# Fourier mixing folded by symmetry in tokens and frequencies, and another order of TensorE fills and modulation blocks inside the attention loop

## The chip, the cores and the metric

The kernel runs on one core of one Trainium2 chip. The metric is the device time of one execution in microseconds (us). Engine names are those of the profile: PE is TensorE (PEld its weight loads), DVE is VectorE, ACT is ScalarE, POOL is GpSimd, SP the engine that issues most transfers. L957 is line 957 of the kernel before.

## What is computed

A transformer block with mixture-of-experts, followed by two state-space layers, all in float32. Only one piece of the first block matters here:

```
hl = modulate(rms_norm(x, g), shift, scale)        # 512 tokens x 1024
pl = hl @ w_in                                     # q, k, v (512 wide each) and f (512 wide)
attention: 4 heads, each q block of 128 tokens against 768 keys, difference of two softmaxes
fourier_mix(f):
    fg = f.reshape(b, n, 4, 128)                   # 4 groups of 128 channels
    fr = fft2(fg, axes=(tokens, channels), norm='ortho').real
    return einsum('bngc,gcd->bngd', fr, w_fourier)
x = x + gate * (concat([attention, fourier]) @ w_out)
```

For real input, the real part of the two-dimensional transform is the sum of cosine times cosine and minus sine times sine. A cosine over the 512 tokens is even about token 256, a sine odd; the same holds of the result's frequencies.

## The kernel before

Activations lie features-major: 128 partitions of features by 512 tokens. The kernel is one block of hand-ordered instruction streams, one for each engine, joined by semaphores; each engine runs its stream in order, so a wait holds everything behind it.

**The attention loop** has 16 iterations n = 0 to 15 (head n // 4, query block n % 4). In each one:

- PE runs `scores(n)` (L931, 4 matmuls into banks 2 to 5), which waits until ACT has taken the exponentials of n - 1. Then come the two halves of `turn_weights(n - 1)` (L943, three 128x128 transposes each), and between and behind them **fills**: projections of the values and of the Fourier features (`values`, `to_mix`, both L840, 8 matmuls of 512 columns), the Fourier work, a head's `head_values` (L957, 3 matmuls in each of two iterations), its `head_norm_sum` (L964), and the start of the output projection (`out_part`, L969).
- DVE runs `maxima(n)` (L2234 and L2237), which waits for the scores; two **modulation blocks** (`mod_block`, L2230); `attention_weights(n)` (L2242, L2244, L2248), which waits for ACT's exponentials; and a third block. In some iterations there is also a head's evacuation (`head_out`, L2252), its variance (`head_var`, L2256) or its scaling (`head_scale`, L2260 and L2263, a reciprocal over 512 columns).
- ACT takes the exponentials (L1664) and copies PE's results out of PSUM (`copy`, L1553), in a fixed order, with a square root (L1682) for a head's norm where n = 8, 12 and after the loop.

**Modulation blocks** compute the conditioning vector of the second block: 48 blocks of 128 rows by 1024, each one a multiply with accumulation on DVE over 512 KB of weights. Two buffers hold them. POOL issues a block's load (L613) as soon as DVE has used the block two before it. The rule is three blocks in each iteration.

**The ring** holds projection weights in two slots of 2 MB. SP refills a slot (L427) as soon as PE is done with it; in the loop these are the two slots of the output projection's weights, the first one free after `values(5)` (n = 3), the second after `to_mix(3)` (n = 7).

**Fourier work of a group g**: `mix_channels` (L900) multiplies 4 token tiles by a 128x256 table of cosines and sines; ACT copies the two banks; `mix_tokens` (L908 and L909) sums over the 4 token tiles, 8 matmuls of 512 columns; ACT copies; `mix_out` (L916) applies the group's weights. It stands in n = 8 to 14.

After the loop come the last head, the output projection, the router and the experts. The loads of the expert weights start when the last head's values are done (`pv_mm`) and all 48 blocks are used (`ada_used`).

Of the kernel before, what the change touches and what calls it, by code (L numbers as in the profile page):

```python
# [19 lines left out]
ALU = mybir.AluOpType  # L20
# [3 lines left out]
P = 128  # L24
D = 1024
KC = D // P
T = 512
TC = T // P
# [57 lines left out]
def build(nc, A, out):  # L86

    with ExitStack() as ctx:
# [53 lines left out]
        dft_c, dft_s, dft_ch = wk(13312, TC, T), wk(15360, TC, T), wk(17408, 256)  # L142
        fab, fre = wk(17664, 2, 4, 256), wk(19712, T)
# [114 lines left out]
        B_BANKS = (0, 2, 0, 2, 5, 2, 5, 5)  # L258
        SCATTER_BANKS = (7, 4)
# [43 lines left out]

        def f32r(v):

            return bass.AP(twins[v.tensor.name][v.offset // TWIN], v.offset % TWIN, [(TWIN, P), *v.ap[1:]])
# [24 lines left out]
        fourier_mm, fourier_evac = sem("fourier_mm"), sem("fourier_evac")  # L331
        AB, FR, FO = 2, 3, 4
# [5 lines left out]
        zero_row_stored, route_mm = sem("zero_row_stored"), sem("route_mm")  # L338
# [75 lines left out]
        def _(sp):  # L414
# [34 lines left out]
            for name, tile in (("rope_c", rope_c), ("rope_s", rope_s), ("dft_c", dft_c), ("dft_s", dft_s),  # L449
# [8 lines left out]
                         zeros[0:1, :].unsqueeze(1).broadcast_to([1, 4, 256])).then_inc(zero_row_stored, 16)  # L458
# [9 lines left out]
            for n in range(TILES_E):  # L468
# [9 lines left out]
                elif n == 8:  # L478
                    sp.wait_ge(routing_evac, 5)
                    sp.dma_start(h_rows[0:T, :].rearrange("(t p) d -> p t d", p=P), tok_rows).then_inc(rows_stored, 16)  # L480
                    sp.wait_ge(rows_stored, 16)
# [118 lines left out]
        def _(pool):  # L600
# [15 lines left out]
            pool.wait_ge(zero_row_stored, 16)  # L616
            pool.wait_ge(rows_stored, 16)
# [98 lines left out]
        def _(pe):  # L716
# [174 lines left out]
            def mix_channels(g):  # L891
                if g:
                    pe.wait_ge(fourier_evac, 4 * (g - 1) + FR)
                else:
                    pe.wait_ge(in_mix, 16 * 6)
                    pe.wait_ge(qkv_evac, 22)
                for t in range(TC):
                    if g and t == 2:
                        pe.wait_ge(fourier_evac, 4 * (g - 1) + FO)
                    mm = nc.tensor.matmul(PS[:, t // 2, (t % 2) * 256:(t % 2 + 1) * 256], fT[:, g, t * P:(t + 1) * P],  # L900
                                          dft_ch, start=True, stop=True)
                    if t % 2:
                        mm.then_inc(fourier_mm, 1)

            def mix_tokens(g, tiles):
                pe.wait_ge(fourier_evac, 4 * g + AB)
                for t in tiles:
                    nc.tensor.matmul(PS[:, 0, :], fab[:, g % 2, t, 0:P], dft_c[:, t, :], start=(t == 0), stop=False)  # L908
                    mm = nc.tensor.matmul(PS[:, 0, :], fab[:, g % 2, t, P:2 * P], dft_s[:, t, :], start=False,  # L909
                                          stop=(t == TC - 1))  # L910
                if t == TC - 1:
                    mm.then_inc(fourier_mm, 1)

            def mix_out(g):
                pe.wait_ge(fourier_evac, 4 * g + FR)
                nc.tensor.matmul(PS[:, 1, :], wfour[:, g, :], fre, start=True, stop=True).then_inc(fourier_mm, 1)  # L916
# [58 lines left out]
            for n in range(HEADS * TC):  # L975
                hd, qc = n // TC, n % TC
                scores(n)
                if n in (9, 11, 12, 14):
                    mix_out({9: 0, 11: 1, 12: 2, 14: 3}[n])
# [7 lines left out]
                elif n == 1:  # L987
                    values(2)
                    values(3)
                elif n == 2:  # L990
                    values(4)
                elif n == 3:
                    values(5)
                    tile_done()
                    tile_wait("in", 1, 1)
                elif n < 8:
                    to_mix(n - 4)
                    if n == 7:
                        tile_done()
                elif n in (8, 9, 11, 12):  # L1000
                    mix_channels({8: 0, 9: 1, 11: 2, 12: 3}[n])
                elif n in (10, 13):
# [2045 lines left out]
```

## Time and profile before

| | |
|---|---|
| median of 3 runs | 2228.44 us (2226.58 to 2231.45) |
| the profiled execution | 2228.12 us |
| its span, first to last instruction | 2226.4 us |
| granted TensorE clock, mean | 0.991 |
| PE busy / DVE busy / ACT busy | 96% / 54% / 32% |
| attention loop, first scores to the last turn of weights | 117.7 to 294.8 us |

The profile is of one execution. Its span is 1.7 us shorter than that execution's device time; what lies around the span is taken as unchanged. Matmuls overlap in the list of instructions, so the time of one in a stream is read from the start of the next one, or from the chain of waits, whose pieces do not overlap.

### The profile page before, as it was taken

The page shows a single profiled execution, that of the slowest core. Times are in us where ns is not written, and L with a number is a line of the kernel's source. Part 1 is how long each engine was busy: PE and PEld are TensorE (multiplying, and loading weights), DVE is VectorE, ACT ScalarE, POOL GpSimd, SP SyncE. Part 2 cuts the span into 40 slices and gives each one's busy share as a digit, 9 for nine tenths or more (in the row PEclk, how much of TensorE's full clock was granted, in tenths as well). Part 3 has the DMA queues.
Part 4 walks back from the last instruction along what each step waited for, and adds up shares of the span by engine and source line. Part 5 has one row for each costly group of instructions (what it writes and reads, how often), then busy time and mean ns, then how long its engine had stood idle before and what let it go on. Part 6 is the DMA issues. An engine that isn't in the chain of part 4 may idle for free.

```text
span 2226.4 us, 24806 instructions
## 1 busy us (share of the span) xinstructions
PE 2136.7 (96%) x9914; PEld 1429.5 (64%) x9914; DVE 1211.9 (54%) x1726; ACT 702.7 (32%) x1059; POOL 154.2 (7%) x157
## 2 busy tenths in 40 slices
PE   7999998997999989999999999999999999999998
PEld 3444444333333336678888888877777788888886
DVE  1876853344443336894465555576876545343434
ACT  4123422110000006223332232256785424231321
POOL 0011100003210014000000000000110000000000
PEclk9999999999999999999999999999999999999999
DMA  9756464999999992212354545314342222222221
GB/s 389 288 188 214 144 253 188 414 427 427 420 427 426 426 422 93 77 67 76 132 180 151 184 162 182 125 57 129 113 148 86 95 78 93 95 94 94 94 95 57
DMA packets 112808, 434.71 MB, mean 195 GB/s; under 512 B 7982, under 2 KB 13106, under 8 KB 98760
## 3 DMA queue, kind: packets, MB, share of 16 engines
q1 hardware_dynamic: 92872, 361.46, 42.4%
q0 software_dynamic: 19840, 71.93, 9.0%
q8 instruction: 66, 1.08, 0.2%
q14 instruction: 30, 0.25, 0.0%
HBM read 430.57 MB, written 6.36 MB: 196 GB/s over the span
## 4 chain that ended last, share of the span: by engine, by line
PE 58%; PEld 14%; DVE 8%; issue 7%; DMA 6%; ACT 3%; DVEq 2%; POOL 1%; POOLq 0%; SPq 0%; PEldq 0%; ACTq 0%
PE PS L1132 8%; PE PS L740 6%; PE PS L743 6%; PE PS L744 6%; PE PS L840 6%; PEld PS L740 4%; PEld PS L744 4%; PEld PS L743 4%; PE PS L1155 4%; DMA work<-in_w_dn 3%; PE PS L1399 2%; PE PS L1403 2%; PE PS L1402 2%; PE PS L1169 2%; PE PS L969 2%
## 5 line engine op out<-in xcount | busy, mean ns | idle before, releaser
L744 PE MATMUL PS<-work_f32r,work_f32r 128*128 128x512 f32 x1168 | 454.4, 389 | 0.0
L2155 DVE TENSOR_TENSOR ring_f32r<-ring,work_f32r 128x2048 fp32r<-128x2048 f32 x100 | 227.8, 2287 | 140.5 <-ACT work_f32r L1553 140.1
L740 PE MATMUL PS<-work_f32r,work_f32r 128*128 128x512 f32 x768 | 299.5, 390 | 2.0 <-DVE work_f32r L2900 1.0
L743 PE MATMUL PS<-work_f32r,ring_f32r 128*128 128x512 f32 x768 | 298.8, 389 | 0.0
L1553 ACT ACTIVATE work_f32r<-ring 128x2048 fp32r<-128x2048 f32 x100 | 190.3, 1910 | 303.1 <-DMA ring<-in_mlp_w 246.6
L744 PEld LDWEIGHTS PS<-work_f32r,work_f32r 128*128 128x128 f32 x1168 | 219.2, 188 | 45.7
L1132 PE MATMUL PS<-work 128*64 128x512 f32 x752 | 171.2, 598 | 1.7 <-ACT work L1761 1.7
L740 PEld LDWEIGHTS PS<-work_f32r,work_f32r 128*128 128x128 f32 x768 | 144.2, 188 | 33.1 <-DVE work_f32r L2900 1.5
L743 PEld LDWEIGHTS PS<-work_f32r,ring_f32r 128*128 128x128 f32 x768 | 144.2, 188 | 30.0 <-issue 0.2
L740 PE MATMUL PS<-h_f32r,work_f32r 128*128 128x512 f32 x400 | 155.9, 390 | 1.5 <-DVE work_f32r L2175 1.5
L743 PE MATMUL PS<-h_f32r,ring_f32r 128*128 128x512 f32 x400 | 155.6, 389 | 0.0
L2472 DVE SCALAR_TENSOR_TENSOR x<-PS,mod,x 128x512 f32<-128x512 f32 x128 | 90.2, 746 | 68.7 <-PE PS L1169 68.3
L1771 ACT ACTIVATE work<-PS 128x256 f32<-128x256 f32 x32 | 12.3, 383 | 357.7 <-PE PS L1132 357.7
L2717 DVE SCALAR_TENSOR_TENSOR x<-PS,mod,x 128x512 f32<-128x512 f32 x64 | 48.1, 751 | 137.0 <-PE PS L744 136.9
L1399 PE MATMUL PS<-h_f32r,work_f32r 128*128 128x512 f32 x288 | 122.4, 425 | 0.0
L1132 PEld LDWEIGHTS PS<-work 128*64 128x64 f32 x752 | 51.6, 137 | 101.6 <-issue 101.6
L1553 ACT ACTIVATE work<-PS 128x512 f32<-128x512 f32 (+2 forms) x94 | 50.8, 550 | 198.5 <-PE PS L840 85.8
L1402 PE MATMUL PS<-h_f32r,ring_f32r 128*128 128x512 f32 x288 | 113.3, 393 | 0.0
L1403 PE MATMUL PS<-work_f32r,work_f32r 128*128 128x512 f32 x288 | 113.3, 393 | 0.0
L2708 DVE TENSOR_SCALAR work<-PS 128x512 f32<-128x512 f32 x64 | 43.9, 691 | 116.3 <-PE PS L744 116.2
L1155 PE MATMUL PS<-work 128*64 128x512 f32 x384 | 94.9, 611 | 9.1 <-DMA work<-in_w_dn 8.4
L1925 ACT ACTIVATE work_f32r<-work 128x512 fp32r<-128x512 f32 x64 | 40.4, 631 | 171.8 <-DVE work L2708 171.8
(423 smaller groups left out, 3358.7 us busy)
## 6 DMA issues: line engine op xcount, KB each, us to landing
work<-in_w_gu SPq DMA_DIRECT2D x47, 2048.0 KB, 20.4
ring<-in_mlp_w SPq DMA_DIRECT2D x64, 1024.0 KB, 5.1
work<-in_w_dn SPq DMA_DIRECT2D x24, 2048.0 KB, 23.7
ring<-in_w_gu SPq DMA_DIRECT2D x16, 2048.0 KB, 24.8
work<-in_ada_w_2T POOLq DMA_DIRECT2D x48, 512.0 KB, 3.6
work<-in_ada_w_2T POOLq DMA_DIRECT2D x16, 1536.0 KB, 6.8
ring<-in_m_w_in SPq DMA_DIRECT2D x20, 1024.0 KB, 5.1
work<-in_w_adaT POOLq DMA_DIRECT2D x8, 2048.0 KB, 10.3
```

The costliest lines, as they stand in the source:

```text
L740: mm = nc.tensor.matmul(PS[:, bank + k, :], f32r(w_of), f32r(hi(c)), start=first and c == 0, stop=False)
L743: nc.tensor.matmul(PS[:, bank + k, :], f32r(wlo), f32r(hi(c)), start=False, stop=False)
L744: mm = nc.tensor.matmul(PS[:, bank + k, :], f32r(w_of), f32r(lo(c)), start=False, stop=last and c == 3)
L840: mm = nc.tensor.matmul(PS[:, bank, 0:n], cols_of(c), rhs_of(c), start=(c == 0), stop=(c == KC - 1))
L1132: mm = nc.tensor.matmul(PS[CAP * half:CAP * (half + 1), 2 + s, :], xbT[:, 4 * part + c, CAP * s:CAP * (s + 1)], w[:, c, half * 512:(half + ...
L1155: mm = nc.tensor.matmul(PS[CAP * s:CAP * (s + 1), 5 + n, :], hidT[:, s, k % 2, CAP * (k // 2):CAP * (k // 2 + 1)], tiles[s][0][:, k, n * 5 ...
L1399: mm = nc.tensor.matmul(PS[:, k, :], f32r(w_of), f32r(h[:, c, :]), start=(c == 0), stop=False)
L1402: nc.tensor.matmul(PS[:, k, :], f32r(wlo), f32r(h[:, c, :]), start=False, stop=False)
L1403: mm = nc.tensor.matmul(PS[:, k, :], f32r(w_of), f32r(xbc_h_lo[:, c, :]), start=False, stop=(c == KC - 1))
L1553: return nc.scalar.activation(out, in_, ACT.Copy)
L2155: tt(f32r(ring[:, s, at, :]), ring[:, s, at, :], f32r(tiles[s][:, at, :]), ALU.subtract).then_inc(w_split, 1)
L2472: stt(x[:, c, :], PS[:, SCATTER_BANKS[c % 2], :], mod1[:, 5 * KC + c:5 * KC + c + 1], x[:, c, :], ALU.mult, ALU.add).then_inc(x2_added, 1)
```

## The change

- **Tokens folded.** After a group's features are projected, DVE forms for the token pairs (t, 512 - t) the difference into `f_odd` and the sum in place (`fold_tokens`, two operations of 255 columns, one operand read backwards, and a copy of token 256). PE then transforms only 2 tiles of sums by cosines and 2 tiles of differences by sines, with token 256 added by one more matmul: 5 matmuls of 128 columns.
- **Frequencies folded.** `mix_tokens` computes only the cosine sum at 257 frequencies and the sine sum at 255: 3 matmuls of 257 columns and 2 of 255. ACT copies the first, and DVE makes frequencies 1 to 255 as their sum and 257 to 511 as their difference (`unfold_frequencies`, two operations of 255 columns, one written backwards). `mix_out` waits for this instead of for ACT's copy.
- **Fills in another order.** n = 1 held two value projections, now one; n = 1 to 4 hold values 2 to 5, n = 5 to 8 the four Fourier projections, and n = 9 to 12 one Fourier group each, with `mix_out` of a group in the next iteration. Three matmuls of the output projection move from n = 15 to n = 13.
- **Modulation blocks in another order**: 2, 3, 3, 3, 4, 5, 5, 4, 1, 3, 3, 2, 0, 3, 4, 3 for n = 0 to 15 (before, 3 each), at most two of them ahead of `attention_weights`. `fold_tokens` stands behind `maxima` in n = 6 to 9, `unfold_frequencies` at the end of n = 9 to 12.
- The tables of the token transform are smaller (386 KB and 255 KB instead of 1024 KB each). A store of a zero row signals on another semaphore.

The diff, cut to its core:

```diff
@@ TensorE
             def mix_channels(g):
+                pe.wait_ge(folded, g + 1)
                 if g:
-                    pe.wait_ge(fourier_evac, 4 * (g - 1) + FR)
+                    pe.wait_ge(fourier_evac, 3 * (g - 1) + FO)
...
-                for t in range(TC):
-                    mm = nc.tensor.matmul(PS[:, t // 2, (t % 2) * 256:(t % 2 + 1) * 256], fT[:, g, t * P:(t + 1) * P],
-                                          dft_ch, start=True, stop=True)
+                even, odd, cosines, sines = fT[:, g, :], f_odd[:, g, :], dft_ch[:, 0:P], dft_ch[:, P:2 * P]
+                for t in range(2):
+                    nc.tensor.matmul(PS[:, 0, t * P:(t + 1) * P], even[:, t * P:(t + 1) * P], cosines, start=True, stop=True)
+                nc.tensor.matmul(PS[:, 0, 3 * P:4 * P], odd[:, P:2 * P], sines, start=True, stop=True)
+                nc.tensor.matmul(PS[:, 0, 2 * P:3 * P], odd[:, 0:P], sines, start=True, stop=False)
+                nc.tensor.matmul(PS[:, 0, 2 * P:3 * P], f_half[:, g, :], cosines, start=False, stop=True).then_inc(fourier_mm, 1)
+            def mix_tokens(g):
+                pe.wait_ge(fourier_evac, 3 * g + AB)
+                if g:
+                    pe.wait_ge(folded, GROUPS + g)
+                for t in range(3):
+                    nc.tensor.matmul(PS[:, 1, 0:257], fab[:, g % 2, t, :], dft_c[:, t, :], start=(t == 0), stop=(t == 2))
+                for t in range(2):
+                    mm = nc.tensor.matmul(PS[:, 1, 257:512], fab[:, g % 2, 2 + t, :], dft_s[:, t, :], start=(t == 0), stop=(t == 1))
             def mix_out(g):
-                pe.wait_ge(fourier_evac, 4 * g + FR)
+                pe.wait_ge(folded, GROUPS + g + 1)
@@ ScalarE
-                if n in (8, 9, 11, 12):
-                    mixed_channels({8: 0, 9: 1, 11: 2, 12: 3}[n])
+                if FIRST_MIX <= n < FIRST_MIX + GROUPS:
+                    mixed_channels(n - FIRST_MIX)
                 exps(n)
@@ VectorE
+            def fold_tokens(g):
+                dve.wait_ge(qkv_evac, 18 + g + 1)
+                early, late = fT[:, g, 1:T // 2], mirrored(fT[:, g, T // 2 + 1:T])
+                tt(f_odd[:, g, 1:T // 2], early, late, ALU.subtract)
+                nc.vector.tensor_copy(f_half[:, g, 0:1], fT[:, g, T // 2:T // 2 + 1])
+                tt(early, early, late, ALU.add).then_inc(folded, 1)
+            def unfold_frequencies(g):
+                dve.wait_ge(fourier_evac, 3 * g + UV)
+                early, late, odd = fre[:, 1:T // 2], mirrored(fre[:, T // 2 + 1:T]), PS[:, 1, 257:512]
+                tt(late, early, odd, ALU.subtract)
+                tt(early, early, odd, ALU.add).then_inc(folded, 1)
+            BLOCKS_AT = (2, 3, 3, 3, 4, 5, 5, 4, 1, 3, 3, 2, 0, 3, 4, 3)
...
-                mod_block(3 * n)
-                mod_block(3 * n + 1)
+                first, count = sum(BLOCKS_AT[:n]), BLOCKS_AT[n]
+                ahead = min(2, count) if n else 0
+                for q in range(first, first + ahead):
+                    mod_block(q)
                 attention_weights(n)
-                mod_block(3 * n + 2)
+                for q in range(first + ahead, first + count):
+                    mod_block(q)
                 if hd >= 2 and qc == 0:
                     head_scale(hd - 2)
+                if FIRST_MIX <= n < FIRST_MIX + GROUPS:
+                    unfold_frequencies(n - FIRST_MIX)
```

Two places show what moves. The first is DVE in iteration n = 12, from its maxima to the next iteration's. Before (the rows with `mod` are modulation blocks, `norm_buf` is the head's variance and reciprocal):

```order
L2234 TENSOR_REDUCE sm<-PS 128x2
L2237 TENSOR_SCALAR sm<-sm 128x2
L2256 TENSOR_SCALAR norm_buf<-PS 128x512
L2230 SCALAR_TENSOR_TENSOR work,mod<-work,cond 128x1024 x2
L2242 RECIPROCAL sm<-sm 128x2
L2244 TENSOR_SCALAR work<-work,sm 128x768
L2248 SCALAR_TENSOR_TENSOR work<-work,sm 128x768
L2230 SCALAR_TENSOR_TENSOR work,mod<-work,cond 128x1024
L2260 RECIPROCAL norm_buf<-norm_buf 128x512
L2263 SCALAR_TENSOR_TENSOR h<-work,sm,norm_buf 128x512
```

and of the change:

```order
L2222 TENSOR_REDUCE sm<-PS 128x2
L2225 TENSOR_SCALAR sm<-sm 128x2
L2244 TENSOR_SCALAR norm_buf<-PS 128x512
L2230 RECIPROCAL sm<-sm 128x2
L2232 TENSOR_SCALAR work<-work,sm 128x768
L2236 SCALAR_TENSOR_TENSOR work<-work,sm 128x768
L2248 RECIPROCAL norm_buf<-norm_buf 128x512
L2251 SCALAR_TENSOR_TENSOR h<-work,sm,norm_buf 128x512
L2263 TENSOR_TENSOR work<-work,PS 128x255
L2264 TENSOR_TENSOR work<-work,PS 128x255
```

The three blocks have left this iteration, and group 3's unfold stands behind the head's scaling.

The second is PE from `scores(12)` to `scores(13)`. Before (L931 scores, L916 mix out, L943 transposes, L900 channels, L908 and L909 tokens):

```order
L931 MATMUL PS<-work 128x512 x2
L931 MATMUL PS<-work 128x256 x2
L916 MATMUL PS<-work 128x512
L943 MATMUL PS<-mats_sb,work 128x128 x3
L900 MATMUL PS<-work 128x256 x4
L943 MATMUL PS<-mats_sb,work 128x128 x3
L908 MATMUL PS<-work 128x512
L909 MATMUL PS<-work 128x512
L908 MATMUL PS<-work 128x512
L909 MATMUL PS<-work 128x512
L931 MATMUL PS<-work 128x512 x2
```

and of the change, up to the next iteration's mix out (L922), which waits for the unfold above:

```order
L937 MATMUL PS<-work 128x512 x2
L937 MATMUL PS<-work 128x256 x2
L922 MATMUL PS<-work 128x512
L949 MATMUL PS<-mats_sb,work 128x128 x3
L905 MATMUL PS<-work 128x128 x2
L906 MATMUL PS<-work 128x128
L907 MATMUL PS<-work 128x128
L908 MATMUL PS<-work 128x128
L949 MATMUL PS<-mats_sb,work 128x128 x3
L915 MATMUL PS<-work 128x257 x3
L917 MATMUL PS<-work 128x255 x2
L937 MATMUL PS<-work 128x512 x2
L937 MATMUL PS<-work 128x256 x2
L922 MATMUL PS<-work 128x512
```

All of a group's token sums now stand in its own iteration, and between them and the next `mix_out` there is only one `scores`.

## Rows read from the trace of the kernel before

**Rows 1.** By stretch: length, busy of PE, PEld, DVE, ACT, POOL, clock, DMA, GB/s.

```profile
212.90:275.20 62.30, 60.35 (x207) 30.28 (x206) 49.91 (x67) 30.73 (x57) 9.14 (x17) 1.00 0.48 167
275.20:294.80 19.60, 19.31 (x62) 8.74 (x62) 17.05 (x28) 7.43 (x16) 3.44 (x7) 1.00 0.56 189
400.00:600.00 200.00, 188.00 (x854) 73.33 (x853) 84.53 (x180) 26.14 (x57) 34.46 (x24) 0.98 1.01 425
```

**Rows 2.** Chain of waits, PE pieces: start, us, what (two records a matmul).

```profile
187.48 2.58 PE PS L957 x6
203.77 6.88 PE PS L840 x16
212.97 1.49 PE PS L931 x8
214.94 1.74 PE PS L900 x8
216.71 0.61 ACT work L1553
225.98 1.05 PE PS L916 x2
```

**Rows 3.** Chain of waits, pieces on DVE, the transfers and ACT.

```profile
163.38 3.51 DMA work<-in_ada_w_2T
168.44 7.98 DMA work<-in_ada_w_2T
...
262.16 1.88 ACT work L1664 x4
...
267.23 3.26 DVE norm_buf L2260
...
294.83 0.52 PE PS L943 x3
```

**Rows 4.** PE groups by shape, first 350 us: xcount | busy us, mean ns.

```profile
L840 PE MATMUL PS<-work,ring 128*128 128x256 f32 x64 | 14.1, 379 | 0.0
L729 PE MATMUL PS<-ones 128*128 128x128 f32 x32 | 4.7, 289 | 0.1
```

**Rows 5.** DVE in order of time: start, us, engine, line, what [idle before].

```profile
57.72 2.77 DVE L2132 TENSOR_TENSOR work<-work,norm_buf 128x256 f32<-128x256 f32 x8
141.13 1.75 DVE L2234 TENSOR_REDUCE sm<-PS 128x2 f32<-128x1536 f32 x1
143.04 1.22 DVE L2230 SCALAR_TENSOR_TENSOR work<-work,cond 128x1024 f32<-128x1024 f32 x1
146.15 0.16 DVE L2242 RECIPROCAL sm<-sm 128x2 f32<-128x2 f32 x1
148.09 1.22 DVE L2230 SCALAR_TENSOR_TENSOR work<-work,cond 128x1024 f32<-128x1024 f32 x1
224.50 3.35 DVE L2260 RECIPROCAL norm_buf<-norm_buf 128x512 f32<-128x512 f32 x1
228.60 1.75 DVE L2234 TENSOR_REDUCE sm<-PS 128x2 f32<-128x1536 f32 x1
```

**Rows 6.** The block loads: issue to landing, all 48; and DVE's first block.

```profile
DMA to landing us min/median/max: 3.4/3.6/8.0
134.99 1.22 DVE L2230 SCALAR_TENSOR_TENSOR work<-work,cond 128x1024 f32<-128x1024 f32 x1 [2.06 <-DMA work<-in_ada_w_2T]
```

**Rows 7.** PE in order of time: `scores` of iteration 5.

```profile
177.12 1.56 PE L931 MATMUL PS<-work 64*128 64x512 f32 x8
```

**Rows 8.** Issues in order of time: SP's ring load, POOL's first blocks, ACT's table load.

```profile
167.33 44.52 SPq L427 DMA_DIRECT2D ring<-in_w_out  x4
131.02 1.45 POOL L613 DMA_DIRECT2D work<-in_ada_w_2T  x2 [23.35 <-DVE work L2141]
219.46 1.28 ACT L1682 ACT_TABLE_LOAD   x1
```

**Rows 9.** Waits, first 350 us: us in total, times, longest.

```profile
DVE work L2230 <- DMA work<-in_ada_w_2T: 18.0, 15, 3.7
```

More of the change, by code:

```diff
@@ L914, in mix_out @@
             def mix_out(g):
-                pe.wait_ge(fourier_evac, 4 * g + FR)
-                nc.tensor.matmul(PS[:, 1, :], wfour[:, g, :], fre, start=True, stop=True).then_inc(fourier_mm, 1)
+                pe.wait_ge(folded, GROUPS + g + 1)
+                nc.tensor.matmul(PS[:, 0, :], wfour[:, g, :], fre, start=True, stop=True).then_inc(fourier_mm, 1)
             def scores(n):
@@ L977, in _ @@
                 scores(n)
-                if n in (9, 11, 12, 14):
-                    mix_out({9: 0, 11: 1, 12: 2, 14: 3}[n])
+                if FIRST_MIX < n <= FIRST_MIX + GROUPS:
+                    mix_out(n - FIRST_MIX - 1)
                 if n:
@@ L986, in _ @@
                     values(1)
[L987 to L998, printed above, removed]
-                        tile_done()
-                elif n in (8, 9, 11, 12):
-                    mix_channels({8: 0, 9: 1, 11: 2, 12: 3}[n])
-                elif n in (10, 13):
-                    mix_tokens({10: 1, 13: 3}[n], range(2, 4))
+                elif n < 5:
+                    values(n + 1)
+                    if n == 4:
+                        tile_done()
+                        tile_wait("in", 1, 1)
+                elif n < FIRST_MIX:
+                    to_mix(n - 5)
+                    if n == 8:
+                        tile_done()
+                elif n < FIRST_MIX + GROUPS:
+                    mix_channels(n - FIRST_MIX)
+                elif n == 13:
+                    tile_wait("out", 0, 0)
+                    pe.wait_ge(fourier_evac, 3 * 2 + FO)
+                    out_part(0, 1, OUT_ORDER[0:3])
                 elif n == 14:
-                    tile_wait("out", 0, 0)
                     pe.wait_ge(head_done, 2)
+                    pe.wait_ge(fourier_evac, 3 * 3 + FO)
                     out_part(0, 0, OUT_ORDER[0:5])
                 elif n == 15:
-                    pe.wait_ge(fourier_evac, 4 * GROUPS)
-                    out_part(0, 1, OUT_ORDER[0:6])
+                    out_part(0, 1, OUT_ORDER[3:6])
                 if n:
@@ L1017, in _ @@
                     head_values(hd - 1, 3, KCH)
-                if n in (8, 11):
-                    mix_tokens({8: 0, 11: 2}[n], range(4))
-                elif n in (9, 12):
-                    mix_tokens({9: 1, 12: 3}[n], range(2))
+                if FIRST_MIX <= n < FIRST_MIX + GROUPS:
+                    mix_tokens(n - FIRST_MIX)
                 elif n == 15:
@@ L2269, in _ @@
                     modulation((5, ADA_TILES // 2), -MOD_EARLY // 4, cond1, col("b_ada", 0, 48), mod1)
-                    attention_weights(0)
-                    for q in range(3):
-                        mod_block(q)
-                    continue
+                    nc.vector.memset(f_odd[:, :, 0:1], 0.0)
+                    nc.vector.memset(f_half, 0.0)
+                if FIRST_MIX - 3 <= n < FIRST_MIX + 1:
+                    fold_tokens(n - FIRST_MIX + 3)
                 if hd >= 2 and qc == 0:
```

81 lines of the change are left out of this document (32 added, 49 removed).

## The prediction

> **What bounds the kernel now.** I read the busy time by stretch first. In the Fourier part of the loop (212.9 to 275.2 us) PE is busy 60.4 of 62.3 us, and DVE already 49.9; in the stretch behind it 19.3 and 17.1 of 19.6 [rows 1]. So PE is full, but DVE has a fifth of its time free at most. The chain of waits says the same more sharply: up to 261 us it runs almost only over PE pieces [rows 2], then over DVE, ACT's exponentials and block loads until the last turn of weights at 294.83 [rows 3]. The last three iterations are thus bound by DVE and its loads, with PE just kept fed. Further on, the experts stream their weights at 425 GB/s with the transfer engines at 1.01 [rows 1]; these loads begin when the loop's last values and blocks are done. No part of the rest depends on absolute time, so what the loop gains or loses is what the kernel gains or loses. Everything comes down to one number: when the last turn of weights (now 294.83) starts.
>
> **What PE saves.** A full matmul of 512 columns costs 0.86 us (8 in 6.88, 3 in 2.58), one of 256 columns 0.43 (4 in 1.74) [rows 2]. Before, a group takes 4 x 0.43 + 8 x 0.86 = 8.6 us before its `mix_out`. After, it takes 2.2 us for the tokens (3 of 257 and 2 of 255 columns; 256 columns in a long row cost 14.1 / 32 = 0.44) and 5 of 128 columns, 4.7 / 16 = 0.29 each, 1.5 us [rows 2, 4]. That is 4.9 us less per group, 19.8 us for four. For the small ones the price is bounded by 0.29 (same weights again) and the 0.43 of twice the columns, so 1.5 to 2.2 us; I take 1.5.
>
> **What DVE gets.** In start-to-start times DVE's pieces are: `maxima` 1.9, a block 1.15, `attention_weights` 1.94 (146.15 to 148.09), `head_scale` 4.1 (224.50 to 228.60) [rows 5]. A two-operand operation over 256 columns costs 2.77 / 8 = 0.35 [rows 5]. A fold is two of these and a tiny copy, 0.8 us; an unfold 0.7; together 6 us in the loop. No row shows an operand read or written backwards: below, a forward one at 0.35 is the floor; above, I take 1.0 us, one third of the 3.26 of the slowest pass over 512 columns, the reciprocal [rows 3], scaled to 255 with a margin down since it is no division. I take 0.35, the row of the same operation.
>
> **What the blocks can do.** There are two buffers. From the end of a block to the start of the one two later it takes 0.3 us to POOL's issue and 3.4 to 3.6 to the landing, a **trip** of 3.8 us [rows 3, 6]. Two blocks per iteration are always there; more than two wait for trips. So five blocks cost two trips: an iteration with five takes at least 1.9 + 0.8 + 3 x 1.15 + 2 x 3.8 = 13.8 us on DVE, while PE needs 1.49 (scores) + 0.7 (turns) + 6.88 (projection) + 2.58 (values) = 11.7 [rows 2]. DVE falls behind just where the change puts the most blocks.
>
> **The walk.** M(n) is when DVE starts `maxima(n)`.
> - `scores(5)` started at 177.12 [rows 7]. It comes one projection of 6.9 us earlier, less about 0.5 of waiting for `attention_weights(1)`, and ends near 172.4: M(5) = 172.4.
> - n = 5: the ring slot frees when `values(5)` ends, and SP's load starts with it, as at 167.33 before [rows 8]. Then a block load issued just behind took 8.0 us instead of 3.5 [rows 3]. Now this lands in an iteration with five blocks: the first starts at 179.2; with three blocks and two trips M(6) = 190.2.
> - n = 6: as above, 13.8. M(7) = 204.0.
> - n = 7: 1.9, fold 0.8, `head_out` 0.6, a block, a trip, two blocks: 10.6. M(8) = 214.6. PE also idles some 4 us here, as `head_norm_sum` needs this late `head_out`.
> - n = 8: ACT's square root stands behind the copies of the last projection, which is late too: `head_scale` begins at 222.3. M(9) = 226.4, 5 us behind its scores.
> - n = 9: 1.9, fold, two blocks, a trip, a block, unfold: M(10) = 235.9. PE has reached `mix_out(0)` at 231.6 and waits 4 us.
> - n = 10: PE-bound: `mix_out` 1.0, a wait for its copy 0.4, channels 1.5, turns 0.7, values 2.58, tokens 2.2, scores 1.49 [rows 2]: 10.0. M(11) = 245.9.
> - n = 11: a loop without slack: `mix_out` 1.0, copy 0.6, channels 1.5, copy 0.6 (216.71), exponentials 1.88, weights 1.94, unfold 0.7, handoffs 0.5: 8.8 [rows 2, 3]. M(12) = 254.7. (ACT takes group channels before the exponentials.)
> - n = 12: the same up to the exponentials, then square root with table load 1.9 (1.28 of it the load [rows 8]), `head_scale` 4.1, unfold: 13.1. M(13) = 267.8; PE idles 5 us before `mix_out(3)`.
> - n = 13: `mix_out`, two copies, table load, exponentials, weights, a block: 8.5. M(14) = 276.3. n = 14: four blocks, 9.9. M(15) = 286.2. n = 15: maxima, `head_out`, two blocks (one on a trip), weights: done at 293.1.
>
> The same walk over the order of before ends 1.1 us too early against the trace, mostly in n = 13 to 15; I have already put that in by rounding each step up. So 294.83 becomes 293.1: a gain of 1.7 us. Of the 19.8 us that PE saves, some 18 turn into waits for DVE. Other edits cost nothing: the smaller tables land before 60 us, where PE waits for none of them; the row store's semaphore is passed long before it is used. The sum is 2228.12 - 1.7 = **2226.4 us**, against the profiled execution, which lies 0.3 under the median. A measurement of this kernel can tell about 0.2% (4.5 us) from no change, so this is no change.
>
> On the trip, the Trainium skill ("DMA: Bandwidth & Descriptors", Anatomy of one DMA) gives 2.0 us plus the bytes at 436 GB/s. For 512 KB that is an estimate of 3.2 us where the rows show 3.4 to 3.6 [rows 6]; by it the trip would be 3.5 and the walk end 3 us earlier, at 2223.6.
>
> **The rivals.**
> - *The ring load doesn't collide.* The first of the five blocks' loads is issued about a microsecond from the ring load's start; a little earlier and it lands before. Then n = 5 costs 4.4 us less, all of it on the walk: 2222.0. Against it: the same engine order gave 8.0 us before. For it: the margin is under 1 us, and the walk has other steps that I rounded up.
> - *PE is the bound.* DVE is busy 54% of the span and PE 96%; if DVE's lateness is absorbed, all 19.8 us come through: 2208.3. For it: the PE row of the stretch, and that PE hardly waited before. Against it: the last iterations already hang on DVE [rows 3], and the DVE work of n = 5 to 15 (97 us by the pieces above, without trips) is as long as PE's (99). The Trainium skill says to improve the most-contended engine ("Perfetto Trace Analysis", Identifying the Most-Contended Engine); by occupancy that is PE here, and by that rule this rival is the forecast.
> - *Slower: the trip gets longer.* Where blocks are taken back to back, two loads are always in flight. At the loop's start POOL issued two at 131.02, and the first was used at 134.99, 3.97 later, not 3.5 [rows 6, 8]. About twelve trips lie one behind another on the walk, so each 0.1 us costs 1.2 us. From a trip of 4.3 us on the kernel is measurably slower; at 4.4 it is 2233.6. Against it: before, pairs issued 1.15 apart landed in 3.5.
> - *Slower: backwards operands.* At 1.0 us instead of 0.35 for each of the 16 operations the walk grows by 8.9 us: 2235.3. It decides from about 0.8 us each.
>
> **How the numbers follow.** The walk's result 0.50 (its own range 2223.7 to 2231.5, from the small matmuls' upper price of +2.8 and a trip 0.1 to 0.2 us off); no collision or a part of the lateness absorbed 0.23; PE the bound 0.10; longer trips 0.13; slow backwards operands 0.04. Faster by over 0.2%: 0.33, within 0.50, slower 0.17. The range leaves out the PE-bound case and the far end of the slow ones: 2217 to 2233.
>
> **What would show it.** Right: PE idle of some 15 us in n = 7 to 13, with the releaser DVE, at `head_norm_sum(0)`, `mix_out(0)` and `mix_out(3)`; DVE waits for block loads well over the 18.0 us of before [rows 9], one of some 5 us near 174 to 179; iterations n = 5 and 6 17 to 18 and 14 us long on DVE. Wrong: PE over 97% busy from 212 on; scores of n = 6 to 9 followed at once by their maxima; folds or unfolds over 0.5 us an operation; trips of other than 3.8 us; or a last turn of weights before 289 or after 298.

## The result, and the profile after

| | before | after |
|---|---|---|
| median, 20 runs each | 2228.57 us (2226.55 to 2232.54) | 2233.8 us (2229.82 to 2237.77) |
| the profiled execution / its span | 2228.12 / 2226.4 | 2237.49 / 2235.5 |
| mean granted clock | 0.991 | 0.983 |
| last turn of weights | 294.83 | 302.32 |

The ratio is 1.0021 (95% interval 1.0014 to 1.0027): slower by 0.2%. The forecast was 2226.4 in a range of 2217 to 2233, so the time lies just outside it, 7.4 us above the forecast. The profiled execution of after is a late one of its own kernel, 3.7 us over the median, and its mean clock of 0.983 is among the lowest of the 20 (their median is 0.985); what it shows of single places is real, but its sum is larger than that of a typical run. That will matter below. Nor is the rest of the kernel quite fixed: from the last turn of weights to the end of the span it took 1931.6 us in the profile before, 1933.2 after, and 1928.6 to 1935.9 in all fourteen profiles of this study. A gain read at the last turn of one profile is therefore not yet a gain of the kernel; for that the medians count.

Busy time by stretch, after, the same three stretches as [rows 1] (length, busy of PE, PEld, DVE, ACT, POOL, clock, DMA share, GB/s):

```profile
212.90:275.20 62.30, 51.07 (x198) 28.50 (x197) 48.77 (x72) 24.79 (x48) 6.61 (x12) 0.88 0.43 143
275.20:294.80 19.60, 19.60 (x62) 9.27 (x61) 13.44 (x22) 8.08 (x15) 3.30 (x6) 0.91 0.43 142
400.00:600.00 200.00, 188.42 (x860) 73.18 (x858) 81.80 (x176) 26.53 (x58) 33.69 (x24) 0.98 1.00 424
```

PE had 60.4 us of work in the first stretch before and has 51.1 now, part of it at a slower clock: it idles 11 us. The experts' stretch is what it was. The kernel is no longer bound by PE in the loop.

The chain of waits of after, some pieces (start, us, what). Before, it ran mostly over PE up to 261 us [rows 2], except for DVE and two block loads from 159.95 to 179.76 [rows 3]; now block loads stand in it from the start of the loop:

```profile
130.40 5.00 DMA work<-in_ada_w_2T
...
136.96 4.36 DMA work<-in_ada_w_2T
...
169.35 4.58 DMA work<-in_ada_w_2T
...
175.49 8.16 DMA work<-in_ada_w_2T
...
197.09 3.57 DMA work<-in_ada_w_2T
...
202.22 3.49 DMA work<-in_ada_w_2T
...
211.84 2.07 PE PS L970 x2
...
227.59 3.35 DVE norm_buf L2248
231.03 0.77 DVE h L2251
231.93 5.46 PE PS L963 x6
...
244.82 4.98 DMA work<-in_ada_w_2T
...
271.99 0.75 DVE h L2251
...
273.46 2.07 PE PS L922 x2
...
289.15 4.80 DMA work<-in_ada_w_2T
```

Two things stand out. Loads of 512 KB that took 3.5 us take 4.4 to 5.0 in several places, and 8.2 once, beside the ring load. And one `head_norm_sum` (L970) and one `mix_out` (L922) take 2.07 us where 1.05 is normal [rows 2], three matmuls of `head_values` (L963) 5.46 instead of 2.58.

The waits of the loop, 117 to 300 us (us in total, times, longest), against 18.0 us for block loads before [rows 9]:

```profile
DVE work L2218 <- DMA work<-in_ada_w_2T: 23.4, 20, 4.5
PE PS L970 <- ACT work L1675: 5.8, 2, 4.1
PE PS L922 <- DVE work L2264: 5.6, 2, 5.0
PE PS L949 <- DVE work L2236: 4.1, 3, 1.9
PE PS L963 <- DVE h L2251: 3.4, 1, 3.4
```

The last four are idles of PE, and behind the longest one of each line the granted clock is low. Four windows that begin with the first matmul after the idle (the clock is the third number from the end), and the loop as a whole:

```profile
211.84:217.40 5.56, 5.56 (x14) 2.38 (x14) 3.65 (x7) 0.33 (x1) 1.51 (x3) 0.50 0.57 189
231.93:237.20 5.27, 5.27 (x7) 2.17 (x8) 5.12 (x11) 2.25 (x5) 0.73 (x2) 0.50 0.27 103
273.46:276.00 2.54, 2.54 (x6) 1.40 (x7) 2.46 (x3) 0.43 (x1) 0.00 (x0) 0.50 0.00 0
144.60:153.60 9.00, 8.94 (x20) 4.00 (x21) 8.00 (x12) 2.36 (x5) 1.71 (x3) 0.81 0.59 211
117.70:302.30 184.60, 161.68 (x529) 78.66 (x527) 141.14 (x224) 62.84 (x127) 27.02 (x48) 0.94 0.50 171
```

0.50 is the lower of PE's two levels, 1.2 GHz. Before, the clock was 1.00 in all of 117.7 to 294.8. So this kernel pays an idle of PE twice: once for the wait, and again for the 2.7 us by which norm sum, scores and a turn are longer at 211.84, or the 2.9 us of `head_values` at 231.93 (5.46 instead of 2.58). The Trainium skill ("TensorE: Matmul & The Clock Gate", A second HAM failure mode: psum-queue depth-cycling) says as much: waits between bursts throw the clock back, and the throughput suffers though each matmul at full clock is as fast as ever. It also calls the number of slow matmuls at a kernel's start variable from run to run (What's actually happening). The place of a fall varied here too, between kernels: with four buffers, below, the same idle before `head_values(1)` was followed by the full clock (three matmuls in 2.81 us), and a shorter one before `mix_out(0)` by the low one:

```profile
221.32 2.81 PE L965 MATMUL PS<-work 128*128 128x512 f32 x6 [3.39 <-DVE h L2254]
...
229.90 2.04 PE L924 MATMUL PS<-work 128*128 128x512 f32 x2 [2.10 <-DVE work L2267]
```

The length of a single idle thus does not settle by itself what the clock does behind it.

### The profile page after: what moved, and what is told of

Read it like the earlier page. It is cut to its first block, busy times and chain, and to the rows that moved or that the text cites. A ratio compares the mean times of both kernels' runs of the same rounds, so it can differ in the third digit from the quotient of the medians.

```text
span 2235.5 us, 24794 instructions
## 1 busy us (share of the span) xinstructions
PE 2131.7 (95%) x9898; PEld 1431.6 (64%) x9898; DVE 1218.0 (54%) x1748; ACT 699.5 (31%) x1055; POOL 153.8 (7%) x157
## 4 chain that ended last, share of the span: by engine, by line
PE 55%; PEld 15%; DVE 9%; issue 7%; DMA 7%; ACT 3%; DVEq 2%; POOL 1%; POOLq 0%; SPq 0%; PEldq 0%; ACTq 0%
PE PS L1133 8%; PE PS L745 6%; PE PS L748 6%; PE PS L749 6%; PEld PS L745 5%; PEld PS L749 5%; PEld PS L748 4%; PE PS L845 4%; PE PS L1156 4%; DMA work<-in_w_dn 3%; PE PS L1400 2%; PE PS L1404 2%; PE PS L1403 2%; PE PS L1170 2%; PE PS L975 2%
## 5 line engine op out<-in xcount | busy, mean ns | idle before, releaser
L1554 ACT ACTIVATE work<-PS 128x512 f32<-128x512 f32 (+3 forms) x90 | 47.5, 539 | 195.2 <-PE PS L845 75.9
## 6 DMA issues: line engine op xcount, KB each, us to landing
ring<-in_w_gu SPq DMA_DIRECT2D x16, 2048.0 KB, 23.4
```

Of the source, the lines that this page charges most:

```text
L1554: return nc.scalar.activation(out, in_, ACT.Copy)
```

## The experiments

All twelve kernels were run beside the kernel before, whose medians in them lay between 2228.2 and 2229.8 us. "Under after" compares medians of different batches of runs. Where the ratios to the kernel before give another difference it is named, and a difference of under some 2.5 us between two of these kernels is not clear of the intervals.

**Keeping the clock.** Ahead of the longest waits of PE stand small matmuls on ones, in a free bank.

```diff
+                    if n in (1, HEADS * TC - 1):
+                        keep_warm(6, 6 if n == 1 else 5)
                     pe.wait_ge(a_ready, n + 1)
...
+                if hd == 0:
+                    keep_warm(1, 12)
                 pe.wait_ge(osq_ready, hd + 1)
...
+                        if hd == 1:
+                            keep_warm(1, 11)
                         pe.wait_ge(head_done, hd)
...
+                if g == GROUPS - 1:
+                    keep_warm(0, 16)
                 pe.wait_ge(folded, GROUPS + g + 1)
```

> The changed kernel with dummy 128-column matmuls before five of PE's waits (the turn of weights 1 and 15, the norm sum of head 0, the values of head 1, the mix out of group 3), so that PE does not stand idle there. Theory: the waits themselves cost what the walk says, and the 9 us by which the loop ends later than the walk come from the granted TensorE clock of 0.5 behind each of these waits; the kernel gets 4 to 8 us faster, the clock stays at 1.0 in the loop, and the last turn of weights starts near 295. Rival: VectorE sets the pace anyway, and the slow matmuls lie beside its work; no change within 1 us. Second rival: the dummies push real work back by up to 1 us and nothing is won.

Measured: 2232.93 us (12 runs), ratio to before 1.0010 (0.9999 to 1.0021). In its profile the clock is 1.00 from 117 to 200 and 0.98 from 200 to 290 (0.98 and 0.89 in after's), and the last turn comes at 297.79, 4.5 us earlier than in after's profile. But the median is only 0.9 us better (2.5 by the ratios, and the two intervals overlap). The profile of after is of a run with more clock lost than its median run. So the clock's price is 4 to 6 us between these two profiles (4.5 at the last turn, 5.9 in the length of the loop) and an estimated 1 to 2.5 in a typical run, as long as the kernel also waits for its blocks; block waits did not fall (24.7 us).

**Four block buffers instead of two.** The kernel before has no room for them; the smaller tables of the change free it. The semaphores of the two added buffers, and the later counts on them, are left out here.

```diff
-        ..., [wk(26624, D), wk(27648, D)]
+        ..., [wk(17664, D), wk(18688, D), wk(26624, D), wk(27648, D)]
...
-                pool.wait_ge(ada_used, 2 + ADA_LATE + max(q - 1, 0))
-                pool.dma_start(ada_block[q % 2], ...).then_inc(ada_loaded[q % 2], 16)
+                pool.wait_ge(ada_used, 2 + ADA_LATE + max(q - 3, 0) if q > 1 else 2)
+                pool.dma_start(ada_block[q % 4], ...).then_inc(block_loaded[q % 4][0], 16)
```

> The changed kernel with four buffers for modulation blocks instead of two, same order. Theory: VectorE falls behind in iterations 4 to 7 because five blocks cost two round trips of 3.8 us (4.9 us for the second load of a pair); with four buffers its waits for block loads fall from 24 us to under 6, PE's idle before the norm sum of head 0 goes from 4.1 to about 1, and the kernel gets 8 to 14 us faster (the walk without clock loss gives 8, the rest is clock). Rival: VectorE's own work, not the loads, is what is late; under 3 us.

Measured: 2222.18 us (8 runs), 0.9968 (0.9957 to 0.9979): 11.6 us less than after, and faster than before. Waits, 117 to 300 us:

```profile
PE PS L924 <- DVE work L2267: 7.1, 2, 5.0
PE PS L965 <- DVE h L2254: 3.4, 1, 3.4
DVE work L2221 <- DMA work<-in_ada_w_2T: 1.7, 2, 1.4
```

Of 23.4 us of block waits 1.7 are left, and `head_norm_sum(0)` waits 0.88 us instead of 4.09. The idles before `mix_out(3)` and `head_values(1)` are as long as in after (L924 is `mix_out`, L965 `head_values`), and one of 2.1 before `mix_out(0)` is new.

**Three blocks in every iteration, in the changed kernel**, `BLOCKS_AT = (3,) * 16`.

> The changed kernel with three modulation blocks in each iteration, as before the change. Theory: the order of the blocks costs, since five in a row wait for loads; by the walk it is worth 1.5 us, and 3 to 6 with the clock. But three blocks in iterations 8 and 12, where the head's scaling stands, delay the unfold and make PE's waits there longer, so a loss of up to 3 us is the other side. Rival: the order of blocks was right and this is 3 us slower or more.

Measured: 2229.28 us (12 runs), 0.9999 (0.9990 to 1.0007). Without the new order of blocks, the sum of all that folding and new fills gain and cost is nothing. DVE waits for blocks 14.6 us.

**The new order of blocks alone, in the kernel before.**

> The kernel before with only the new order of modulation blocks (2, 3, 3, 3, 4, 5, 5, 4, 1, 3, 3, 2, 0, 3, 4, 3), no fold and the old fills. Theory: the walk gives 5 to 7 us slower than before, since with five blocks the round trips make VectorE late and PE waits. Rival: with the unfolded Fourier work PE has enough to cover it, within 1.5 us of before.

Measured: 2235.05 us (8 runs), 1.0032 (1.0018 to 1.0045). The same table of numbers costs 5 to 7 us here and 4.5 to 5 in the changed kernel, by the run above. DVE waited 27.3 us for blocks instead of the 18.0 of [rows 9].

**Short trips, before and after.** The question left was whether a trip weighs more now than it did. 46 of the 48 loads bring 8 KB instead of 512, in both kernels.

```diff
+                cols = D if q < 2 else 16
-                pool.dma_start(ada_block[q % 2], A["ada_w_2T"][0, q * P:(q + 1) * P, :]) ...
+                pool.dma_start(ada_block[q % 2][:, 0:cols], A["ada_w_2T"][0, q * P:(q + 1) * P, 0:cols]) ...
...
-                stt(w, w, 1.0, cond2[:], ...
+                stt(w, w, 0.0, cond2[:], ...
```

> The kernel before with short trips: of 48 block loads the first two are whole, the other 46 bring 16 columns of each row (8 KB instead of 512 KB), and the blocks multiply by 0, so the second block's conditioning vector is its bias alone. Same instructions, two buffers, same order; a trip gets shorter by up to the 1.5 to 2 us that the bytes take. Theory (the kernel before has PE as its bound up to 261 us and hides its trips; only the last iterations hang on them): a gain of 1 to 4 us, 2225 to 2228.5. Rival (DVE waits for loads cost before as much as after): a gain like that of the changed kernel with the same edit.

> The changed kernel with the same edit (46 of 48 block loads bring 16 columns of each row, blocks multiply by 0, so the second block's conditioning vector is its bias alone). Two buffers, the change's own order of blocks. Theory (the folded kernel hangs on trips of 3.8 to 5 us, some twelve of them on its chain in n = 1 to 11): the waits for blocks fall from 24.0 to some 10 us, and 8 to 12 us come back, 2222 to 2226, so that with short trips the change is faster than the kernel before by 2 us or more, the other way round than with the real ones. Rival (the idles and clock of PE cost the change, not the loads): under 4 us come back.

Measured: before 2227.02 (10 runs), 0.9992 (0.9982 to 1.0002); after 2222.14 (7 runs), 0.9971 (0.9960 to 0.9983). The same edit is worth 1.9 us before (its interval still includes no change) and 11.7 after (11.1 by the ratios). DVE's waits fell by about as much in both. First the kernel before, with the transfers (KB each, median us from issue to landing):

```profile
DVE work L2231 <- DMA work<-in_ada_w_2T: 3.1, 2, 2.1
...
work<-in_ada_w_2T POOLq DMA_DIRECT2D x46, 8.0 KB, 1.9
```

and the changed one:

```profile
DVE work L2219 <- DMA work<-in_ada_w_2T: 5.6, 5, 1.4
...
work<-in_ada_w_2T POOLq DMA_DIRECT2D x46, 8.0 KB, 1.9
```

15 us of DVE waits vanish in the one and 18 in the other, with gains of 1.9 and 11.7: before, PE's work covers nearly all of them, after, about a third. This is the central measurement of the study. Shorter loads also take traffic off the transfer engines (the ring load's median landing falls from 9.2 to 6.3 us), but four buffers, which leave every load whole, come to the same time (2222.18), so it is the trip that counts. On the landing of 1.9 us for 8 KB the trace agrees with the fixed part of about 2 us that the Trainium skill gives ("DMA: Bandwidth & Descriptors", Anatomy of one DMA).

**No arithmetic in folds and unfolds.** Each keeps a copy of one column and its signal.

```diff
-                tt(f_odd[:, g, 1:T // 2], early, late, ALU.subtract)
-                nc.vector.tensor_copy(f_half[:, g, 0:1], fT[:, g, T // 2:T // 2 + 1])
-                tt(early, early, late, ALU.add).then_inc(folded, 1)
+                nc.vector.tensor_copy(f_half[:, g, 0:1], fT[:, g, T // 2:T // 2 + 1]).then_inc(folded, 1)
...
-                tt(late, early, odd, ALU.subtract)
-                tt(early, early, odd, ALU.add).then_inc(folded, 1)
+                nc.vector.tensor_copy(late[:, 0:1], odd[:, 0:1]).then_inc(folded, 1)
```

> The change without the arithmetic of the folds and unfolds on DVE: the two additions of each are left out, a copy of one column stays and signals, and the two buffers are zeroed once in iteration 0, so the Fourier half of the output is not that of the reference. The small matmuls, the order of fills and blocks stay. Eight folds and unfolds of some 0.75 us each, 6 us of DVE work in the loop. If DVE is the bound throughout n = 5 to 12, 4 to 6 us of it come back: 2228 to 2230. If the block loads are the bound (a trip hides a fold behind a load), 1 to 3 us come back: 2231 to 2233.

Measured: 2232.76 us (12 runs), 1.0021 (1.0011 to 1.0031): 1.0 us under after, at the near end of the second case, and by the ratios (1.0021 for both) nothing. The folds are not what costs the change its gain.

**The norms' steps reordered.** Head 0's square root no longer stands behind a projection's copy, and group 3's unfold stands ahead of head 1's scaling.

```diff
@@ ScalarE
                 elif n < FIRST_MIX:
+                    if n == 8:
+                        head_root(0)
                     projected(13 + n)
...
-                if hd >= 2 and qc == 0:
-                    head_root(hd - 2)
                 if FIRST_MIX <= n < FIRST_MIX + GROUPS:
                     mixed_tokens(n - FIRST_MIX)
+                if n == 12:
+                    head_root(1)
@@ VectorE
-                if hd >= 2 and qc == 0:
-                    head_scale(hd - 2)
                 if FIRST_MIX <= n < FIRST_MIX + GROUPS:
                     unfold_frequencies(n - FIRST_MIX)
+                if hd >= 2 and qc == 0:
+                    head_scale(hd - 2)
```

> The change, with two steps of the heads' norms reordered, same work. On ACT the square root of head 0 stands ahead of the last projection's copy in iteration 8 (before, behind it and behind the turned weights), and the square root of head 1 behind the copy of group 3's token sums in iteration 12; on DVE the unfold of group 3 stands ahead of the scaling of head 1. Theory (PE's idles in front of head_values(1), 3.4 us, and mix_out(3), 5.0 us, and the lower clock behind them are a part of what the change lost): both idles go or fall under 1 us, the last turn of weights comes 4 to 8 us earlier than the 302.3 of the change's profile, and the time falls by 3 to 7 us, to 2227 to 2231. Rival (DVE's chain of blocks and trips sets the end whatever PE's idles do): DVE starts its next maxima at the same moments, the idles move elsewhere, and the time stays within 1.5 us of 2233.8.

Measured with two buffers: 2232.16 us (12 runs), 1.0010 (1.0001 to 1.0018), 1.6 us under after (2.5 by the ratios, the intervals overlap), less than I expected. The idle before `mix_out(3)` fell to 0.56 and that before `head_values(1)` to 1.57, but `mix_out(0)` now waits 2.86 and `head_norm_sum` of heads 0 and 2 wait 3.89 and 3.17: with the blocks late, the idle moves. That is what the rival said, and the time is near its bound of 1.5 us. The last turn does stand at 294.82 in this profile, 7.5 us before that of after's, as the theory had it, but the two profiled runs themselves lie 6.7 us apart where the medians lie 1.6: after's profile is the late one.

> Four block buffers and, in addition, two steps of the heads' norms reordered. On ACT the square root of head 0 stands ahead of the last projection's copy in iteration 8, and the square root of head 1 behind the copy of group 3's token sums in iteration 12; on DVE the unfold of group 3 stands ahead of the scaling of head 1. If the two losses (block trips, idles with a lower clock) add up: four buffers alone gave 2222.2, and the two idles left there (3.4 us in front of head_values(1), 5.0 us in front of mix_out(3), each with matmuls at half speed behind it) are worth a further 3 to 7 us: 2215 to 2219. If they are the same loss seen twice: 2221 to 2223.

Measured with four buffers: 2214.66 us (4 runs), 0.9924 (0.9902 to 0.9947), 7.5 us under four buffers alone (9.8 by the ratios). The same reordering is worth 1.6 us with trips in the way and 7.5 without them, just past the upper end of my 3 to 7. DVE in iteration 8, after, where the scaling of head 0 begins at 227.59, 9 us behind its maxima:

```profile
218.63 1.75 DVE L2222 TENSOR_REDUCE sm<-PS 128x2 f32<-128x1536 f32 x1
...
227.59 3.35 DVE L2248 RECIPROCAL norm_buf<-norm_buf 128x512 f32<-128x512 f32 x1 [2.56 <-ACT norm_buf L1679]
```

and with four buffers and the new order, where it begins 6.3 us behind and waits for nothing:

```profile
205.36 1.76 DVE L2227 TENSOR_REDUCE sm<-PS 128x2 f32<-128x1536 f32 x1 [1.34 <-PE PS L939]
...
211.68 3.35 DVE L2253 RECIPROCAL norm_buf<-norm_buf 128x512 f32<-128x512 f32 x1
```

**Four buffers and a kept clock**, without the reordering.

> Four block buffers, and in front of the three longest waits left on PE (head_values(1), mix_out(0), mix_out(3)) 11, 7 and 16 matmuls of 128 columns on ones into a bank that is free there, so that PE does not idle while it waits. No wait gets shorter by it; only the clock is kept. Theory (the lower clock behind an idle costs some 1 to 3 us each, and these lie on the path): granted clock 1.0 from 118 to 282 us, and 2 to 5 us less than the 2222.2 of four buffers alone. Rival (DVE and ACT set the end, PE catches up anyway): clock 1.0 and the time within 1 us of 2222.2.

Measured: 2218.72 us (5 runs), 0.9954 (0.9941 to 0.9967): 3.5 us under four buffers alone (3.1 by the ratios; the two intervals touch), with a clock of 1.00 through the loop (0.94 from 200 to 290 without the small matmuls). They take none of the work away that PE waits for, so this is the price of the clock. Of the 7.5 us of the reordering, which also had a clock of 1.00, up to about half is thus the clock and the rest the waits themselves; that split was not measured in one kernel.

**Four buffers and reordered norms, three blocks in every iteration.**

> Four buffers and the reordered norms, but three blocks in every iteration as before the change. Theory (the change's order of blocks, few of them in n = 8 to 12 where group work and scaling stand, is right once a block no longer needs a trip): slower than the 2214.7 with the change's order, by 3 to 8 us, since n = 8 to 12 then hold 15 blocks instead of 9, 6.9 us more DVE work where DVE is late. Rival (the order of blocks only matters through trips): within 1.5 us of 2214.7.

Measured: 2219.03 us (5 runs), 0.9952 (0.9938 to 0.9966), 4.4 us slower than with the change's order (6.2 by the ratios; no run of the one kernel is as fast as the slowest of the other). So the order of blocks that costs 4.5 us with two buffers gains 4.4 with four buffers and the reordered norms.

**A refined version.** Blocks 2 4 4 4 4 4 5 3 1 2 3 2 0 3 4 3, and five matmuls on ones ahead of `mix_out(0)`.

> Four buffers and the reordered norms, and blocks in the order 2 4 4 4 4 4 5 3 1 2 3 2 0 3 4 3, that is three more in n = 1 to 3, where PE is the bound and DVE free, and one less in n = 5, 7 and 9; and five matmuls on ones ahead of mix_out(0), where PE still idles 1.6 us. Expected: DVE comes 1 to 2 us earlier in n = 7 to 9, mix_out(0) waits under 1 us, and the time is 0 to 2 us under 2214.7. If four blocks in n = 1 to 3 make their iterations wait for loads, 0 to 3 us above it.

Measured: 2213.65 us (4 runs), 0.9939 (0.9922 to 0.9955), the lowest median, but not to be told from 2214.66 (by the ratios it is the slower of the two). The longest waits of PE in the loop:

```profile
PE PS L953 <- DVE work L2243: 2.2, 2, 1.4
PE PS L907 <- ACT h L1558: 1.4, 3, 0.5
PE PS L974 <- ACT work L1679: 1.2, 2, 0.9
```

It is 20 us faster than the change as made and 14 to 15 faster than the kernel before. Its last turn stands at 278.27, 16.6 us before that of the kernel before, against some 20 us of work that PE was saved; this profile is of a run 3.1 us under its median.

## Why the prediction was wrong

The direction was missed: forecast 2226.4, no change; measured 2233.8.

- **PE's saving: right.** Channels of a group take 1.1 us at full clock (forecast 1.5), tokens 2.26 (2.2), so that the saving is 5.2 us for a group and 20.9 for four rather than 19.8. The list of after, group 0's channels and group 1's tokens:

```profile
226.89 0.61 PE L905 MATMUL PS<-work 128*128 128x128 f32 x4
227.34 0.39 PE L906 MATMUL PS<-work 128*128 128x128 f32 x2
227.56 0.39 PE L907 MATMUL PS<-work 128*128 128x128 f32 x2
227.78 0.39 PE L908 MATMUL PS<-work 128*128 128x128 f32 x2
...
247.36 1.47 PE L915 MATMUL PS<-work 128*128 128x257 f32 x6
248.66 1.02 PE L917 MATMUL PS<-work 128*128 128x255 f32 x4
249.62 0.70 PE L937 MATMUL PS<-work 64*128 64x512 f32 x2
```

- **DVE's pieces: right.** From the start of a fold's operation to the next on DVE it is 0.33 us, forecast 0.35. Operands read or written backwards cost nothing extra (0.41 for the addition of an unfold, all forward), and that rival falls:

```profile
194.84 0.42 DVE L2256 TENSOR_TENSOR work<-work 128x255 f32<-128x255 f32 x1
195.17 0.15 DVE L2257 COPY work<-work 128x1 f32<-128x1 f32 x1
195.24 0.41 DVE L2258 TENSOR_TENSOR work<-work 128x255 f32<-128x255 f32 x1
```

- **"Of the 19.8 us that PE saves, some 18 turn into waits for DVE": right in kind, and the loss was larger.** The trips swallow most of it, as the pair of short trips shows.
- **The walk, step by step.** M(5) was 175.11 instead of 172.4. Then n = 5 took 17.8 us (forecast 17.8, the ring load's collision where it was expected, a wait of 4.55), n = 6 14.0 (13.8), n = 7 11.8 (10.6), n = 8 13.1 (11.8), n = 9 to 11 29.0 (28.3), n = 12 12.7 (13.1), n = 13 11.3 (8.5), n = 14 10.6 (9.9), n = 15 7.2 (6.9). The last turn came 9.2 us later than the walk's 293.1; 3.7 us is what this run lies over the median of its kernel. The larger misses are at M(5) and in n = 7, 8 and 13, and they have two causes.
- **First failed step: "a trip of 3.8 us" for every block.** A load alone, and mostly the first of a pair, did take 3.8 to 4.0 us from the end of a block. The second, issued 1.15 us behind, took 5.0. DVE in n = 6 and 7, after (blocks end 1.15 us after they start):

```profile
196.72 1.23 DVE L2218 SCALAR_TENSOR_TENSOR work<-work,cond 128x1024 f32<-128x1024 f32 x1
...
200.69 1.23 DVE L2218 SCALAR_TENSOR_TENSOR work<-work,cond 128x1024 f32<-128x1024 f32 x1 [0.80 <-DMA work<-in_ada_w_2T]
...
202.85 1.23 DVE L2218 SCALAR_TENSOR_TENSOR work<-work,cond 128x1024 f32<-128x1024 f32 x1 [0.93 <-DMA work<-in_ada_w_2T]
...
205.73 1.22 DVE L2218 SCALAR_TENSOR_TENSOR work<-work,cond 128x1024 f32<-128x1024 f32 x1 [1.64 <-DMA work<-in_ada_w_2T]
```

  The block at 200.69 waits 4.0 us from the end of the one at 195.57 (two before it), the one at 202.85 waits 5.0 from 197.87, the one at 205.73, alone again, 3.9. Trips of 4.8 to 5.4 us stand in n = 1, 4, 6, 7, 10 and 14, always with another load in flight (in n = 10 it is the first of the two that is late, the other having been issued 1.2 us behind it), and three of them are whole pieces of the chain above (4.58, 4.98 and 4.80 from issue to landing instead of 3.5, together 3.9 us; the loads of 5.00 and 4.36 at the loop's start, ahead of where the walk begins, stand in it too). That is the rival of longer trips. Its price at a mean of 4.4 us was 2233.6; I gave it 0.13, saying that pairs before had landed in 3.5, for which there was only the median of all loads. The row that spoke for it, 3.97 at 134.99 [rows 6], showed a pair by itself and was the one to follow. The twelve trips that DVE waited for from 184 to 300 us took 3.8 to 5.4 us, 4.3 in the mean; by the prediction's own 1.2 us for each 0.1 that is an estimate of 2232.4. That the price at 4.4 hits the measured time is in part luck, as the clock had no part in it.
- **Second failed step: there was no term for the clock.** I read off three idles of PE of 4 to 5 us and priced each at its length. In after's profile the projection of n = 2, behind the wait of 1.93 at 144.66, takes 8.73 us instead of 7.03. These 1.7 us are one part of the late M(5). The others are that wait itself, which stands behind the two loads at the loop's start and has 0.5 in the walk, and 0.8 us by which n = 4's last block ends behind the scores; against them, the loop began 1.1 us earlier than before. The square root of n = 8 stands behind a projection that came 2.7 us late by the clock, and n = 13 lost as much behind the 5.04 us before `mix_out(3)`: from there to the end of the scores 11.1 us where the same pieces at full clock make 8.4. The typical run pays less, 0.9 to 2.5 us by the kept clock with two buffers; with the trips gone it is some 3.5.
- **A wait was missed.** `head_values(1)` writes the bank of head 0 and waits for the signal of `head_scale(0)` (`head_done`; L963, 3.39). The walk had PE idle before `mix_out(0)` instead, where it then did not wait at all. The total of the three long idles was near: 4.09, 3.39 and 5.04 us, 12.5 together, forecast some 13. By the code the wait is stricter than it has to be: the last to read that bank is `head_var(0)`, at 221.26, ten us before `head_values(1)` starts, and `head_scale` works on copies. A wait for `head_var`'s signal could take this idle away, or move it, without any reordering; no run tried it.
- **"Other edits cost nothing": not tested apart,** but the change with three blocks each (2229.28) and the kernel before lie within 0.1%. That bounds only the sum: a cost of theirs could hide behind a gain of the folding. These two runs and the one of the blocks alone also say where the last 5 us are: the order of blocks. The forecast had put five blocks on "two trips" in iterations of PE's 11.7 us and had thus seen it, but never asked what the change would be without this order; the answer was no change, and with it, slower.
- **"Almost only over PE pieces up to 261 us" read too kindly.** From 159.95 to 179.76 the chain before already ran over DVE and two block loads, 3.51 and 7.98 us [rows 3], with three blocks in an iteration.
- **"PE is the bound": wrong by 25 us as the kernel stands.** With four buffers, the reordered norms and a few blocks moved it comes true for 14 to 15 of its 19.8 us.

How the 7.4 us over the forecast divide is shown only in part: some 4 us by the second loads on the chain and an estimated 1 to 2.5 by the clock in a typical run; the missed wait and the order around the norms are worth 1.6 to 2.5 by experiment. These overlap and are not to be added strictly.

## What to carry to other kernels

When the busiest engine gets less work, first ask which waits its work had covered: here 15 us of waits for loads cost 1.9 us before, and 18 us of them 11.7 after. Add buffers first, then move work: the same order of blocks lost 4.5 us with two buffers and gained 4.4 with four, and the same reordering of norms gained 1.6 and 7.5. Check, too, that a wait is for the last reader of a buffer and not for a later step. Where a fold makes PE idle between bursts, price the idle with the matmuls behind it at half clock, or cover it with small matmuls, and compare medians, since the clock lost differs from run to run.

## What the runs showed of the hardware

- Behind an idle of PE of 1.9 us the clock was lower once (0.81 over the next 9 us, at 144.66 in after); in the same place a wait of 1.4 us (reordered norms) and waits of 2.4 and 1.8 us shortly after one another (three blocks each) were followed by a projection at full clock (7.03 us). The same 3.39 us before `head_values(1)` cost 2.9 us of slow matmuls in after and none with four buffers.
- Of two 512 KB loads from POOL issued 1.15 us apart, one lands 4.6 to 5.0 us after its issue, not 3.5. With four buffers the median of all 48 was 4.6, and DVE waited 1.7 us for loads in the whole loop.
- A load of 8 KB lands in 1.9 us, one of 512 KB alone in 3.5: the bytes are less than half of a trip of 3.8.
- A row of 255 columns read or written backwards costs a float32 addition on DVE 0.41 to 0.42 us, the same as one with all rows forward (0.41).
